# Compressions of a sparse-attention layer: three products of half the columns instead of four, with the weights summed on VectorE

## What is computed

```
def compress(rows, pe, w1, w2):            # CMP_BLOCK 32, CMP_STRIDE 16, HEAD_DIM 64
    n_chunk = Tk // CMP_STRIDE
    r = CMP_BLOCK // CMP_STRIDE            # 2
    chunks = rows[:, :n_chunk * CMP_STRIDE].reshape(B, n_chunk, CMP_STRIDE, N_KV_HEADS, HEAD_DIM)
    blocks = jnp.concatenate([chunks[:, j:j + n_cmp] for j in range(r)], axis=2) + pe[:, None, :]
    flat = blocks.transpose(0, 1, 3, 2, 4).reshape(B, n_cmp, N_KV_HEADS, CMP_BLOCK * HEAD_DIM)
    return jax.nn.gelu(flat @ w1) @ w2     # w1: 2048 x 256, w2: 256 x 64
k_blk = rms_norm(compress(kc, cmp_pe_k, cmp_w1_k, cmp_w2_k), k_norm[0])
v_blk = compress(vc, cmp_pe_v, cmp_w1_v, cmp_w2_v)
```

## Time and profile before

| what | value |
|---|---|
| time before, median of 3 runs | 915.2 us (914.74 to 916.93) |
| the profiled execution's own time | 918.98 us |
| its span, first to last instruction | 917.0 us |
| mean granted TensorE clock | 0.995 of 2.4 GHz |
| PE busy, share of the span | 98% |
| DVE, ACT, POOL busy | 70%, 22%, 7% |

### The profile page before, as it was taken

The page is one execution under the profiler, slowest core; times in us unless marked ns, Lnnn a source line. Parts: engine busy times, 40 slices in busy tenths (PEclk is TensorE's granted clock), DMA queues, the critical chain, the costliest instruction groups (busy, mean ns, idle before and its releaser), DMA issues.

```text
span 917.0 us, 11484 instructions
## 1 busy us (share of the span) xinstructions
PE 902.1 (98%) x4401; PEld 466.1 (51%) x4401; DVE 644.7 (70%) x1245; ACT 197.8 (22%) x448; POOL 64.5 (7%) x70
## 2 busy tenths in 40 slices
PE   9999999999999999999999999999999999999997
PEld 8856777876554445644434434433343343333543
DVE  7665763767868673655677686686776776768895
ACT  4122211106746202411111111111111110111411
POOL 3010041000000000010000000000000000000000
PEclk9999999999999999899999999999999999999999
DMA  8843733450005776789999999999999999999602
GB/s 290 250 174 85 215 108 126 140 211 1 1 1 150 230 277 243 298 332 415 422 425 424 425 425 426 426 424 426 425 422 422 420 422 421 421 423 396 222 23 75
DMA packets 70075, 262.81 MB, mean 287 GB/s; under 512 B 11818, under 2 KB 37814, under 8 KB 53220
## 3 DMA queue, kind: packets, MB, share of 16 engines
q1 hardware_dynamic: 64768, 250.73, 69.9%
q0 software_dynamic: 4080, 8.93, 2.8%
q10 hardware_dynamic: 1172, 2.40, 0.7%
HBM read 254.95 MB, written 13.08 MB: 292 GB/s over the span
## 4 chain that ended last, share of the span: by engine, by line
PE 85%; DMA 8%; SPq 5%; DVE 1%; issue 1%; ACT 0%; DVEq 0%; ACTq 0%
PE ps L1374 77%; SPq L496 4%; DMA w<-in_w_exp_down 3%; DMA w<-in_w_exp_up 3%; PE ps L1861 2%; PE ps L2132 1%; PE ps L1398 1%; SPq L509 1%; DMA h<-in_x_prompt 1%; PE ps L2173 1%; PE ps L1409 0%; PE ps L1864 0%; PE ps L1664 0%; PE ps L1560 0%; DVE probs L2939 0%
## 5 line engine op out<-in xcount | busy, mean ns | idle before, releaser
L1374 PE MATMUL ps<-w,xe 128*64 128x512 f32 x1024 | 228.1, 596 | 4.2 <-DMA w<-in_w_exp_up 4.2
L3347 DVE TENSOR_TENSOR h<-h,ps 128x1024 f32<-128x1024 f32 x120 | 143.2, 1214 | 105.2 <-PE ps L1374 105.0
L1374 PEld LDWEIGHTS ps<-w,xe 128*64 128x64 f32 x1024 | 70.1, 137 | 143.3 <-issue 133.8
L1374 PE MATMUL ps<-w,hT 128*64 128x512 f32 x504 | 115.4, 599 | 0.5 <-DMA w<-in_w_exp_down 0.5
L1374 PE MATMUL ps<-yk,ST 128*128 128x512 f32 (+1 forms) x320 | 105.2, 431 | 0.1
L1374 PEld LDWEIGHTS ps<-yk,ST 128*128 128x128 f32 (+1 forms) x320 | 48.5, 174 | 56.3 <-issue 27.2
L1316 ACT ACTIVATE sg<-ps 64x256 f32<-64x256 f32 x64 | 24.2, 377 | 244.4 <-PE ps L1374 244.0
L945 POOL DMA_INDIRECT xg<-hn_rows,sidx x32 | 32.0, 1000 | 622.3 <-PE ps L2132 362.0
L1327 ACT ACTIVATE yk<-ps 64x512 fp32r<-64x512 f32 x64 | 38.0, 594 | 146.6 <-PE ps L1374 145.8
L1374 PEld LDWEIGHTS ps<-w,hT 128*64 128x64 f32 x504 | 33.3, 136 | 67.6 <-issue 67.4
L1374 PE MATMUL ps<-xT,wring 128*128 128x272 f32 x192 | 54.5, 408 | 1.3 <-issue 1.3
(11 more groups left out here) (453 smaller groups left out, 1183.7 us busy)
## 6 DMA issues: line engine op xcount, KB each, us to landing
w<-in_w_exp_down SPq DMA_DIRECT2D x27, 2048.0 KB, 27.2
w<-in_w_exp_gate SPq DMA_DIRECT2D x32, 1024.0 KB, 30.1
w<-in_w_exp_up SPq DMA_DIRECT2D x32, 1024.0 KB, 30.4
w<-in_w_exp_gate SPq DMA_DIRECT2D x14, 2048.0 KB, 17.1
w<-in_w_exp_up SPq DMA_DIRECT2D x14, 2048.0 KB, 22.0
w<-in_w_exp_down SPq DMA_DIRECT2D x9, 1024.0 KB, 12.4
wring<-in_w_in SPq DMA_DIRECT2D x12, 512.0 KB, 6.4
h<-in_x_prompt SPq DMA_DIRECT2D x8, 512.0 KB, 6.3
```

The lines of the kernel that those rows point to most:

```text
L1374: return nc.tensor.matmul(out, l, r, start=start, stop=stop, skip_group_check=skip)
L3347: TTn(h[0:r, t, :], h[0:r, t, :], both(b, r), ALU.add).then_inc(S["hadd"], 1)
```

## The change

Columns are split by parity. With x_o the odd chunks, EO = x(2n) − x(2n+1), and OE = x(2n+2) − x(2n+1):

- shared = (Wa + Wb)·x_o, hidden even column = shared + Wa·EO, hidden odd column = shared + Wb·OE.

So each `compress_hidden(i, m)` makes three runs of eight products, of 162, 160 and 162 columns, in place of two runs of eight of 324 and 322. `XT` becomes `XO`, `X_EO` and `X_OE`; `wsum` is a new buffer of Wa + Wb.

- DVE makes Wa + Wb (`weight_sum`, four instructions of 128x1024), the differences (`first_chunks` for keys, a new `chunk_columns` for values), and adds the odd part to the copy of the shared one (`hidden_odd`).
- ACT copies the shared part out of PSUM before PE adds the even part onto it (`hidden_shared`), takes the odd chunks out of PSUM for the values (`chunk_odd`), and makes four gelu instructions per compression instead of two.
- `head_norms(1)`, and with it ACT's second `head_roots(P, 12)`, moves from ahead of `conv_tokens` to behind `hidden_bias(0)`, and `heads_T(1)` moves to behind the third `chunk_T(1, k)`.

```
         def compress_hidden(i, m):
...
+                pe.wait_ge(S["cv_t"], factor_made(("w", i, m)))
+                cols = slice(m * P, (m + 1) * P)
+                for k in range(8):
+                    last = mm(hid_even(m), wsum[:, k, cols], XO[:, k], k == 0, k == 7, True)
+                last.then_inc(S["hid_done"], 1)
+                for k in range(8):
+                    last = mm(hid_odd(i, m), w1s[:, 8 + k, cols], X_OE[:, k, :, 0:XC // 2 - 1], k == 0, k == 7, True)
+                last.then_inc(S["hid_done"], 1)
+                pe.wait_ge(S["kv_copied"], copied_at(("hid", i, m)))
+                for k in range(8):
+                    last = mm(hid_even(m), w1s[:, k, cols], X_EO[:, k], False, k == 7, True)
                 last.then_inc(S["hid_done"], 1)
...
+            def first_chunks(pp):
+                both = (pp, pp + 1)
+                dve.wait_ge(S["X_tr"], pp + 2)
...
+            def chunk_columns(pp):
+                half = NCH // 2
+                if pp == 0:
+                    dve.wait_ge(S["hid_done"], hid_at("even", 0, 0))
+                    V.tensor_copy(XO[:, :, :, half:], XV[:, :, :, 1::2])
+                    TTn(X_EO[:, :, :, half:], XV[:, :, :, 0::2], XV[:, :, :, 1::2], ALU.subtract)
+                    TTn(X_OE[:, :, :, half:XC // 2 - 1], XV[:, :, :, 2::2], XV[:, :, :, 1:XC - NCH - 2:2], ALU.subtract)
+                dve.wait_ge(S["kv_copied"], copied_at(("odd", pp)))
+                x = ps[:, 2 + pp % 2, 0:2 * NCH].rearrange("p (g n) -> p g n", g=NKV)
+                TTn(X_OE[:, pp, :, half - 1:half], XV[:, pp, :, 0:1], XO[:, pp, :, half - 1:half], ALU.subtract)
+                TTn(X_EO[:, pp, :, 0:half], x[:, :, 0::2], XO[:, pp, :, 0:half], ALU.subtract)
+                TTn(X_OE[:, pp, :, 0:half - 1], x[:, :, 2::2], XO[:, pp, :, 0:half - 1], ALU.subtract).then_inc(S["X_ev"], 1)
...
+            def weight_sum(i, m):
+                dve.wait_ge(S["w1_in"], 16 * (i + 1))
+                cols = slice(m * P, (m + 1) * P)
+                TTn(wsum[:, :, cols], w1s[:, 0:8, cols], w1s[:, 8:16, cols], ALU.add).then_inc(S["cv_t"], 1)
+            def hidden_odd(i, m):
+                dve.wait_ge(S["kv_copied"], copied_at(("hid", i, m)))
+                dve.wait_ge(S["hid_done"], hid_at("odd", i, m))
+                out = hid_out(m, 1)[:, :, 0:XC // 2 - 1]
+                TTn(out, out, hid_odd(i, m), ALU.add).then_inc(S["hid_b"], 1)
```

More of the change, by code:

```diff
@@ L172, in build @@
         w1s = at("w1s", [P, 16, CH], RB + 16 * K)
-        XT = at("XT", [P, 8, 2 * XC], RB + 32 * K)
+        XO, X_EO, X_OE = (at(x, [P, 8, NKV, XC // 2], off) for x, off in
+                          (("XO", RB + 32 * K), ("X_EO", RB + 32 * K + 4 * 8 * XC), ("X_OE", 134.25 * K)))
+        wsum = at("wsum", [P, 8, CH], RB + 8 * K)
         kcache = at("kcache", [P, NPG, P], RB)
@@ L399, in build @@
         COPIED = [("khalf", 0), ("khalf", 1), "k11", TP, "sample"] + [(x, r) for r in range(2) for x in ("half", "c22", "c11", "c21", "c12")]
+        COPIED[-1:] = [("hid", 0, 1), ("c12", 1), ("hid", 0, 0)] + [("odd", pp) for pp in range(8)] + [("hid", 1, 0), ("hid", 1, 1)]
         HEADS = (TP, 2, 0, 3, 1)
@@ L1745, in _ @@
                 chunk_T(1, k)
+                if k == 2:
+                    heads_T(1)
             chunk_T(1, 7)
@@ L2564, in window_columns @@
                 V.tensor_copy(kwT[:, t * P:t * P + r], ps[:, 7, P:P + r]).then_inc(S["tr_k"], 1)
[L2566 to L2578, removed]
+            def first_chunks(pp):
+                both = (pp, pp + 1)
+                dve.wait_ge(S["X_tr"], pp + 2)
+                x = {k: ps[:, 2 + k % 2, :].rearrange("p (g n) -> p g n", g=NKV) for k in both}
+                for k in both:
+                    V.tensor_copy(XV[:, k, :, :], x[k][:, :, XC:2 * XC - NCH])
+                for k in both:
+                    last = V.tensor_copy(XO[:, k], x[k][:, :, 1:XC:2])
+                chain(last)
+                for k in both:
+                    TTn(X_EO[:, k], x[k][:, :, 0:XC:2], XO[:, k], ALU.subtract)
+                for k in both:
+                    TTn(X_OE[:, k, :, 0:XC // 2 - 1], x[k][:, :, 2:XC:2], XO[:, k, :, 0:XC // 2 - 1], ALU.subtract).then_inc(S["X_ev"], 1)
@@ L2756, in _ @@
             proj_c12(0)
-            chunk_columns(0, 0)
-            chunk_columns(0, 1)
+            first_chunks(0)
             head_norms(0)
@@ L2761, in _ @@
             window_columns(2)
-            chunk_columns(0, 2)
-            chunk_columns(0, 3)
+            first_chunks(2)
             proj_u3(1)
```

109 lines of the change are left out of this document (76 added, 33 removed).

## The result

| | median | runs | ratio to before, 95% interval |
|---|---|---|---|
| kernel before | 915.46 us | 4 (914.74 to 916.93) | |
| changed kernel | 909.85 us | 4 (909.27 to 910.80) | 0.9938 [0.9920, 0.9955] |

The changed kernel is 5.6 us faster, by the medians; 909.7 was predicted. The three gains average 4.9, so it is partly luck that the forecast and the first median lie only 0.15 us apart; the forecast gain of 5.5, a ratio of 0.9940, lies inside all three intervals.

The account below looks back on a forecast made before the run. PE, busy 98% of the span, was taken as the bound. Products save 8.8 us; waits of 0.4, 2.0 and 0.7 and latencies of 0.2 leave 5.5: 915.2 − 5.5 = 909.7 us, range 906.5 to 913.0.

Parts of the forecast that it names:

- Products: PE's four `compress_hidden`: each falls from 8.69 to 6.50 us at the column rate, saving 8.8 us.
- The rival in which weight loads set the pace: PE's compression products: 192 loads at 0.190 us take 36.5 us against 34.8, total 920.0 us; chance 0.04.
- `first_chunks`: DVE before the keys' compression: 1.85 us instead of 1.08, so PE waits 0.4 us ahead of `heads_T(0)`.
- the bounds for DVE: Upper bounds: 0.1 us more per step-two PSUM subtraction, weight sums 1.5 each; 1.0 us more wait from either.
- Gate columns: Values' third chunk transposes: PE waits 2.0 us, through table load, root, norm and `chunk_columns(0)`; 0.7 without the load.
- Ahead of the values: Before the values' first compression product: PE waits 0.7 us for DVE's queued sums and evacuations.
- Latencies: Semaphore latencies of the new waits: 0.2 us taken off the gain.
- POOL's lock: Keys' second weight sum waits for POOL's value-chunk copy, ends at 90.0, PE wants it at 96.2; no cost.
- The rest of the kernel: After the stage: attention and expert stream move with PE; up weights' wait 4.2 us shows the stream near its limit.
- one sign of being wrong: PE's later stages not all starting 5.5 us earlier; first tile's products were to start near 135.3 instead of 140.9.
- The sum: Whole kernel: 8.8 − 0.4 − 2.0 − 0.7, less 0.2 for latencies: 5.5 us off the 915.2 median.
- Clock: Rival: PE's 2.0 us wait drops its clock to 1.2 GHz, products take 7 us more, 916.7 us; chance 0.04.

Follow-up runs that it names:

- The three gains: Changed kernel, unaltered, measured in three sets against the kernel before: ratios 0.9938, 0.9956 and 0.9951.
- the two later profiles of the changed kernel: Changed kernel run and profiled twice more, unaltered, beside the kernel before: 910.03 us (0.9956) and 910.94 us (0.9951).
- the second profile of before: Kernel before, unaltered, profiled once more: 914.92 us in one run, span 913.0.
- the last version: Changed kernel with three edits: `head_norms(1)` sums and root early, values' weight sums in DVE's gaps, `window_columns(2)` ahead of `proj_u2(1)`: 906.59 us, 0.9908.
- the kernel with the move undone in part: Changed kernel with `head_norms(1)`, its root and `heads_T(1)` moved back, but `window_columns(3)` left behind the gate columns' factors: 915.32 us, 0.9991.
- the run with one wait of 2.07: Changed kernel with `head_norms(1)`, its root, `heads_T(1)` and also `window_columns(3)` back where the kernel before has them: 909.72 us, 0.9944.
- The run with both edits: Changed kernel with `head_norms(1)` sums and root ahead of the gelus, and values' weight sums moved into DVE's gaps: 907.09 us, 0.9921.
- The run with the sums early: Changed kernel with `head_norms(1)` split, its sums ahead of the gate factors and its root ahead of the gelus: 908.91 us, 0.9933.

## Why the prediction held, by its own steps

- **Products.** Right in kind, a little too good in size: 6.60 us instead of 6.50 for each `compress_hidden`, so 4 x 2.09 = 8.4 saved instead of 8.8. (The values' pair was not quite twice 8.69, as the prediction read it, but 17.49; after the change it is 13.27, so the saving is 8.40 by its own rows too.) The rival in which weight loads set the pace falls: loads kept their 0.190 us while records came 0.138 apart, and doubling one of the products showed the same price. Rows of the kernel before settle what the prediction had to bound: the router's 16 records of 36 columns, each with a load of the same kind, take 368.26 − 366.56 = 1.70 us, 0.106 each, so loads can follow each other faster than every 0.138 us.

```profile
L1424 PEld LDWEIGHTS ps<-XO,wsum 128*128 128x128 f32 x64 | 9.0, 190 | 1.1 <-issue 0.8
```

```profile
366.56 1.87 PE L1374 MATMUL ps<-wr,xr 128*128 128x36 f32 x16
368.26 1.12 PE L1398 MATMUL ps<-cst,h 128*128 128x128 f32 x8
```

- **`first_chunks`.** A wait of 0.33 us, forecast as 0.4. The subtractions at step two were no dearer than the rows they were estimated from (0.28 for 128 columns), so the bounds for DVE were never needed.
- **Gate columns.** A wait of 1.79 us, forecast as 2.0, by the chain that was forecast: the table load behind `xh`, the root, the norm. Without the load, 0.37 where 0.7 was worked out. Less the 1.07 us by which the stage began later than on the prediction's clock (90.07 and 89.0), the root started at 106.98 (forecast 106.8) and the bank was free at 110.69 (110.6), while PE wanted it at 108.95 (108.6), 0.2 of that by the dearer products: hence 1.79.
- **Ahead of the values.** A wait of 0.71, forecast as 0.7, by DVE's queue as said, though the trace put it down to issue.
- **Latencies.** The 0.2 was too little, and this is the term that was most off in proportion: the three waits cost 0.52, 2.02 and 0.85 us where their rows say 0.33, 1.79 and 0.71, 0.56 more in all. Most of it is not semaphore latency but overlap. A row counts idle time from the end of the work ahead, and that end overlaps what would follow: eight convolution records last 2.00 us, but the next row starts after 1.84, so 0.16 of a wait behind them is hidden in that row, and 0.17 behind the 396-column product ahead of `heads_T(0)` (2.83 and 2.66), and 0.05 behind `compress_out(0)`. The rest, 0.03 to 0.09 each, is in the transposes next to the wait (a pair takes 0.28 instead of 0.22, four of them 0.52 instead of 0.43).
- **POOL's lock.** The second sum took 2.43 us, absorbed as said. The prediction had overlooked that the first sum would hold up POOL's copy as well; that cost nothing either.
- **The rest of the kernel.** Stream and attention followed PE: the up weights' wait is 4.2 us before and after. Taken by the letter, one sign of being wrong was there in the first pair of profiles: the first tile's products start at 136.82, not near 135.3, and 4.1 us earlier than before instead of 5.5. The stage itself began 1.07 us late, and the two later profiles of the changed kernel (136.16 and 135.98) stand 5.1 and 5.3 us ahead of the second one of before (141.24).
- **The sum.** By these sizes 8.40 − 0.52 − 2.02 − 0.85 = 5.0 us, where 5.5 was forecast, and 4.9 is the mean of the three comparisons. Products 0.4 too good and the added 0.2 of latency 0.36 too small were in part made up by waits forecast 0.27 too long. The prediction left the 3.8 us between its profile and the median alone and took 5.5 off the median; the second profile of before shows that this was right.
- **Clock.** It did not fall at a wait of 1.8 or 2.07 us, but did at 4.85: that rival was wrong for this kernel and right as a mechanism.

## What to carry to other kernels

When PE sheds work, look for what stood hidden behind it on the other engines: here the products gave 8.4 us, 3.4 of them went to waits and their restarts, and the last version won nearly all of that back by moving DVE and ACT instructions into gaps, without removing any work. A table load costs little until it stands between a late operand and the instruction that someone waits for, so a root belongs next to the last root. And when a stage's own length in the trace repeats to 0.01 us, judge edits of one us by it, not by the medians alone.

## What was not expected of the hardware

**The clock behind a long wait.** Windows of the kernel with the move undone in part (window, its length, busy us and instructions of PE, PEld, DVE, ACT and POOL, granted clock, DMA share, GB/s):

```profile
103.00:106.00 3.00, 0.11 (x1) 0.00 (x0) 2.90 (x5) 0.00 (x0) 0.00 (x0) 1.00 0.51 131
106.00:108.00 2.00, 0.05 (x1) 0.08 (x2) 1.77 (x5) 0.00 (x0) 0.00 (x0) 0.79 1.08 372
108.00:109.00 1.00, 1.00 (x5) 1.00 (x6) 0.00 (x0) 0.00 (x0) 0.00 (x0) 0.50 1.08 370
...
113.00:114.00 1.00, 1.00 (x5) 0.88 (x4) 0.13 (x2) 0.44 (x2) 0.00 (x0) 0.50 0.23 63
114.00:116.00 2.00, 2.00 (x11) 1.64 (x11) 0.43 (x3) 0.21 (x2) 0.00 (x0) 1.00 0.49 135
```

PE stood from 103.1 to 107.95. The clock fell to 0.50 (1.2 GHz) while it stood, and stayed there for some 6 us of work: eight records of 272 columns took 3.84 us instead of 2.00. Against the run with one wait of 2.07 the stretch is 5.75 longer, 2.78 by the wait itself and 3.0 by the clock. Around the waits of 1.79 and 2.07 us every window shows 1.00.

**The clock in a stretch where PE never stood.** Behind the router's products (128 x 36 columns) the clock fell in some executions and not in others. The same place in the kernel before's first profile, then in the changed kernel's:

```profile
375.00:378.00 3.00, 3.00 (x5) 1.39 (x6) 2.61 (x9) 2.60 (x5) 0.00 (x0) 0.50 0.99 411
```

```profile
368.00:371.00 3.00, 3.00 (x9) 1.33 (x8) 2.69 (x10) 2.52 (x3) 0.00 (x0) 1.00 1.02 422
```

Five products of 512 columns against nine in 3 us. In the second profiles of both kernels it fell in part there (0.64 and 0.60), so it belongs to neither. Of the fourteen profiles of this case the clock held at 1.00 in this place in eight, fell in part in four and to 0.50 in two. What it costs: from the start of `w2s,hidt` (153.94, 147.16) to the end of the span are 763.1 us in the first profile of before and 761.3 in that of the changed kernel. The run with both edits, whose clock stood at 0.50 there too, has 763.4. The run with the sums early has 763.0: its clock held in this place and fell about 9 us later, behind a wait of PE's of 1.0 us. The second profiles and the run with three edits have 761.3 to 761.4. So a fall costs 1.7 to 2.1 us, or nothing that shows: where the clock held in this place, a wait of PE's of 1.0 us for DVE follows, and in the second profiles that wait is absent instead. It is read from executions that happened to differ, since nothing here set the fall on purpose; what brings it about is left open.

With that the 8.5 us between the first two profiled spans come out: 5.53 in the stretch, 2.71 for the gaps, 1.72 for the dip, less 1.46 by which the stage began later (90.07 against 88.61). Of this, 0.52 is the price of the change's own wait ahead of `heads_T(0)`. The other 0.94 arose further ahead, where nothing was changed; most of it is the row transposes' wait, which was 1.2 instead of 0.3 us and ranged from 0.3 to 2.3 over the runs.
